# Three attention loops by pairs: differential maps subtracted and turned once, indexed and latent values stationary in column halves

## What is computed

```python
# even mixer: indexed attention "a", 8 heads of 64; sel = keys the indexer chose
s = where(valid, q @ k.T * d ** -0.5, -inf)
a = softmax(s) @ v * silu(ag)
r = head_group_norm(retention(q, k, bv)) * silu(bg)      # 4 heads of 128
out = concat([a, r]) @ w_out
# odd mixer: differential "c", 4 heads, two maps each (q, k 64; v 128)
o = causal_attention(qs, ks, concat([v, v]), C_QK_DIM ** -0.5)
c = rms_norm(o[:4] - lam * o[4:], subln) * (1.0 - lam_init) * silu(cg)
# latent "m", 8 heads (q, k 96; v 64)
m = causal_attention(q_full, k_full, kv[..., 64:], 96 ** -0.5) * silu(dg)
out = concat([c, m]) @ w_out
```

## Time and profile before

| | us |
|---|---|
| median of three runs | 2604.29 |
| lowest, highest | 2601.57, 2605.11 |
| span of the profiled execution | 2599.6 |
| PE busy in it | 2539.9 (98%) |
| DVE busy | 1311.2 (50%) |
| ACT busy | 657.8 (25%) |
| indexed loop | 127.6 to 283.6 |
| differential loop | 467.0 to 547.4 |
| latent loop | 549.9 to 632.7 |

### The profile page before, as it was taken

The page is one execution under the profiler, slowest core; times in us unless marked ns, Lnnn a source line. Parts: engine busy times, 40 slices in busy tenths (PEclk is TensorE's granted clock), DMA queues, the critical chain, the costliest instruction groups (busy, mean ns, idle before and its releaser), DMA issues.

```text
span 2599.6 us, 31517 instructions
## 1 busy us (share of the span) xinstructions
PE 2539.9 (98%) x12699; PEld 1731.9 (67%) x12699; DVE 1311.2 (50%) x2535; ACT 657.8 (25%) x1485; POOL 60.1 (2%) x116
## 2 busy tenths in 40 slices
PE   8999999999999999999999999999999999999999
PEld 3487557566588888744545745555555775888886
DVE  6765342544544456424464346657473544344564
ACT  2123232364300000133344042525344002000001
POOL 0000000000000000000000010101020000000000
PEclk9999999999999999999999999999999999999999
DMA  4111222000232221221111221212112321322221
GB/s 159 65 65 66 77 87 85 33 33 33 65 97 65 97 97 67 79 97 53 47 66 68 81 81 65 72 42 82 66 49 100 120 97 65 97 69 94 98 78 69
DMA packets 121032, 196.86 MB, mean 76 GB/s; under 512 B 5212, under 2 KB 61336, under 8 KB 119992
## 3 DMA queue, kind: packets, MB, share of 16 engines
q1 hardware_dynamic: 118848, 180.52, 20.4%
q0 software_dynamic: 1344, 12.19, 1.2%
q10 hardware_dynamic: 696, 2.13, 0.2%
HBM read 187.49 MB, written 7.34 MB: 75 GB/s over the span
## 4 chain that ended last, share of the span: by engine, by line
PE 94%; DVE 3%; ACT 2%; issue 1%; DMA 0%; ACTq 0%; SPq 0%; DVEq 0%
PE psum L542 22%; PE psum L539 15%; PE psum L2503 10%; PE psum L2485 8%; PE psum L422 7%; PE psum L407 6%; PE psum L444 4%; PE psum L2537 3%; PE psum L461 2%; PE psum L1249 2%; PE psum L1229 1%; PE psum L468 1%; PE psum L395 1%; PE psum L1237 1%; PE psum L2429 1%
## 5 line engine op out<-in xcount | busy, mean ns | idle before, releaser
L595 DVE TENSOR_TENSOR arena<-arena,psum 128x512 f32<-128x512 f32 x197 | 135.3, 687 | 357.8 <-PE psum L542 304.5
L2503 PE MATMUL psum<-weight_ring,h_t 128*128 128x512 f32 x640 | 291.4, 598 | 0.5 <-issue 0.5
L542 PE MATMUL psum<-h_t,weight_ring 128*128 128x256 f32 x1120 | 250.2, 379 | 1.2 <-DVE h_t L736 1.0
L542 PEld LDWEIGHTS psum<-h_t,weight_ring 128*128 128x128 f32 x1120 | 212.4, 190 | 30.9 <-issue 2.2
L2485 PE MATMUL psum<-h_t,weight_ring 128*128 128x512 f32 x512 | 232.1, 595 | 0.3 <-issue 0.3
L539 PE MATMUL psum<-weight_ring,arena 128*128 128x256 f32 x992 | 220.5, 379 | 1.5 <-ACT arena L2962 1.5
L539 PEld LDWEIGHTS psum<-weight_ring,arena 128*128 128x128 f32 x992 | 188.3, 190 | 27.9 <-issue 2.4
L2503 PEld LDWEIGHTS psum<-weight_ring,h_t 128*128 128x128 f32 x640 | 116.4, 192 | 116.7 <-issue 115.6
L422 PE MATMUL psum<-h_t,weight_ring 128*128 128x512 f32 x416 | 180.1, 593 | 1.2 <-DVE arena L3215 1.0
L542 PE MATMUL psum<-arena 128*128 128x256 f32 x768 | 169.7, 379 | 0.0
L407 PE MATMUL psum<-weight_ring,h_t 128*128 128x512 f32 (+1 forms) x384 | 163.8, 582 | 0.8 <-ACT arena L2042 0.7
(11 more groups left out here) (439 smaller groups left out, 3409.9 us busy)
## 6 DMA issues: line engine op xcount, KB each, us to landing
weight_ring<-in_ffn_w_in_dram SPq DMA_DIRECT2D x44, 1024.0 KB, 7.4
weight_ring<-in_w_in_dram SPq DMA_DIRECT2D x20, 2048.0 KB, 7.9
weight_ring<-in_ffn_w_out_dram SPq DMA_DIRECT2D x8, 2048.0 KB, 7.7
weight_ring<-in_w_in_even_dram SPq DMA_DIRECT2D x7, 2048.0 KB, 8.3
weight_ring<-in_w_in_odd_dram SPq DMA_DIRECT2D x5, 2048.0 KB, 7.9
weight_ring<-in_w_in_dram SPq DMA_DIRECT2D x8, 1024.0 KB, 7.0
weight_ring<-in_w_branch_gdn_dram SPq DMA_DIRECT2D x4, 2048.0 KB, 7.9
weight_ring<-in_ffn_w_out_dram SPq DMA_DIRECT2D x4, 1536.0 KB, 6.7
```

Of the source, the lines that this page charges most:

```text
L542: ins = pe.matmul(out, w, right[:, k, :], start=first, stop=last)
L595: ins = dve.tensor_tensor(out, other, bank, op)
L2503: last = pe.matmul(bank, act[:, k, t * P:(t + 1) * P], slot[:, k, :], start=(k == 0), stop=(k == KD - 1))
```

## The change

The three loops go by pairs: 16 steps of two maps (`pe_pairs`, `act_pairs`, `dve_pairs`). Both maps are scored, masked and exponentiated; then DVE (`weigh`) divides them by their sums before they are turned. Transposes and values of pair m-2 stand in iteration m.

- `mask(m, r)` on DVE waits for the scores and for the transposes of pair m-2, whose slots it writes.
- In c a pair is the two maps of one head. DVE subtracts them with one instruction, scaled so that one division of the output remains; one map is turned and one multiplied. The subtraction of outputs (L2192) goes.
- In a and m a pair is two heads. Both maps are scaled over nk columns and turned. For the values v is stationary, 64 columns wide, in one column half per head, and the turned map moves, 128 columns; the output comes with features on the partitions. ACT copies it out for the first 12 (a) or 14 (m) pairs, DVE the rest. The outputs of a and m are no longer turned; ag and dg are produced by feature too (stationary and moving swapped in the same stream).
- The output projections read tiles from a list. Even: n_first is 3, the retention's four tiles are turned in between. Odd: n_first is 4, the last four tiles wait for the dg gate, which comes after the loop. The norm's squares are taken at pairs 3 and 4, eight each, the square root at pair 5; both of heads 0 and 1 must be copied before m begins. Fill: 2 half steps of seven in a, 2 or 3 matmuls in c, 2 in each of 12 pairs in m.

The core of the diff; the removed lines of the old functions, which stand above, are left out in most places.

```diff
+
+
+def pe_pairs(K, pe, tag, steps, bufs, beside, behind=None):
+
+    slots, turned = bufs
+    n_steps, base = len(steps), K.pair_base[tag]
+    for m in range(n_steps + 2):
+        i = m - 2
+        if i >= 0:
+            step, kept = steps[i], 2 * (i % 2)
+            pe.wait_ge(K.weights_ready, base + i + 1)
+            for r in range(step["heads"]):
+                bank = pe_fresh(K, pe, (tag, "t", i, r))
+                for kb in range(step["nk"] // P):
+                    last = pe.transpose(bank[:, kb * P:(kb + 1) * P], slots[:, kept + r, kb * P:(kb + 1) * P], K.const("ident"))
+                last.then_inc(K.full_of((tag, "t", i, r)), 1)
+        if m < n_steps:
+            step = steps[m]
+            banks = [pe_fresh(K, pe, (tag, "s", m, r)) for r in range(2)]
+            for r in range(2):
+                pe.matmul(banks[r][:, 0:step["nk"]], step["q"][r], step["k"][r], start=True,
+                          stop=True).then_inc(K.full_of((tag, "s", m, r)), 1)
+        if m <= n_steps:
+            beside(m)
+        if i >= 0:
+            step = steps[i]
+            bank, nkb = pe_fresh(K, pe, (tag, "o", i)), step["nk"] // P
+            for r in range(step["heads"]):
+                pe.wait_ge(K.free_of((tag, "t", i, r)), K.turn((tag, "t", i, r)))
+            for kb in range(nkb):
+                ks = slice(kb * P, (kb + 1) * P)
+                if step["heads"] == 1:
+                    last = pe.matmul(bank[:, 0:P], turned[:, 0, ks], step["v"](kb), start=(kb == 0), stop=(kb == nkb - 1))
+                else:
+                    for r in range(2):
+                        last = pe.matmul(bank[64 * r:64 * r + 64, 0:P], step["v"](kb, r), turned[:, r, ks],
+                                         start=(kb == 0), stop=(kb == nkb - 1))
+            last.then_inc(K.full_of((tag, "o", i)), 1)
+        if behind:
+            behind(m)
+    beside(n_steps + 1)
...
+def act_pairs(K, act, tag, steps, bufs, ahead, beside, evicted=0):
+
+    slots, turned = bufs
     n_steps, base = len(steps), K.att_base[tag]
+    for n in range(n_steps + 3):
+        i = n - 3
+        if 0 <= i < evicted:
+            act.wait_ge(K.full_of((tag, "o", i)), K.turn((tag, "o", i)))
+            act.copy(steps[i]["out"], K.bank((tag, "o", i))[:, 0:P]).then_inc(K.free_of((tag, "o", i)), 1)
+        ahead(n)
+        i = n - 2
+        if 0 <= i < n_steps:
+            nk = steps[i]["nk"]
+            if i:
+                act.wait_ge(K.full_of((tag, "o", i - 1)), K.turn((tag, "o", i - 1)))
+            for r in range(steps[i]["heads"]):
+                act.wait_ge(K.full_of((tag, "t", i, r)), K.turn((tag, "t", i, r)))
+                act.copy(turned[:, r, 0:nk], K.bank((tag, "t", i, r))[:, 0:nk]).then_inc(K.free_of((tag, "t", i, r)), 1)
+        if n < n_steps:
+            nk = steps[n]["nk"]
+            for r in range(2):
+                c = 2 * n + r
+                part = slots[:, 2 * (n % 2) + r, 0:nk]
+                act.wait_ge(K.scores_masked, base + c + 1)
+                act.activation(part, part, ACT.Exp, bias=K.stat[:, 20 + c % 4:21 + c % 4], scale=steps[n]["scale"],
+                               accum_out=K.stat[:, 24 + c % 8:25 + c % 8]).then_inc(K.probs_ready, 1)
+        beside(n)
...
+def dve_pairs(K, dve, tag, steps, bufs, beside, finish):
+
+    slots, _ = bufs
...
+    def weigh(i):
+        step, c = steps[i], 2 * i % 8
+        nk, kept = step["nk"], 2 * (i % 2)
+        dve.wait_ge(K.probs_ready, base + 2 * i + 2)
+        dve.reciprocal(K.stat[:, 32 + c:34 + c], K.stat[:, 24 + c:26 + c]).then_inc(K.one_more("dve"), 1)
+        dve.wait_ge(K.steps["dve"], K.step_n["dve"])
+        first, second = slots[:, kept, 0:nk], slots[:, kept + 1, 0:nk]
+        if step["heads"] == 1:
+            ratio = K.stat[:, 40 + i % 4:41 + i % 4]
+            dve.tensor_scalar(ratio, K.stat[:, 24 + c:25 + c], K.stat[:, 33 + c:34 + c], K.lam[:, 4:5], ALU.mult,
+                              ALU.mult).then_inc(K.one_more("dve"), 1)
+            dve.wait_ge(K.steps["dve"], K.step_n["dve"])
+            dve.scalar_tensor_tensor(first, second, ratio, first, ALU.mult, ALU.add).then_inc(K.weights_ready, 1)
+        else:
+            dve.tensor_scalar(first, first, K.stat[:, 32 + c:33 + c], None, ALU.mult).then_inc(K.one_more("dve"), 1)
+            dve.tensor_scalar(second, second, K.stat[:, 33 + c:34 + c], None, ALU.mult).then_inc(K.weights_ready, 1)
+
+    for n in range(n_steps + 3):
+        if n >= 3:
+            finish(n - 3)
         if n < n_steps:
+            mask(n, 0)
+            mask(n, 1)
+        if 1 <= n <= n_steps:
+            weigh(n - 1)
+        beside(n)
...
+def even_pairs(K, V):
+    for c in range(A_H // 2):
+        for i in range(NT):
+            nk = (i + 1) * P
+            steps.append(dict(q=[V["aq_t"][p:p + 64, c, i * P:nk] for p in (0, 64)],
+                              k=[V["ak_t"][p:p + 64, c, 0:nk] for p in (0, 64)], nk=nk, heads=2,
+                              v=lambda kb, r, c=c: V["av"][:, kb, (2 * c + r) * 64:(2 * c + r + 1) * 64],
+                              scale=A_D ** -0.5, out=V["mixed"][:, c, i * P:nk]))
...
+    pe_pairs(K, pe, "a", even_pairs(K, V), V["pairs"], lambda m: half_step(2 * m), lambda m: half_step(2 * m + 1))
+
+    def rest():
+        for i in range(12, 16):
+            pe.wait_ge(K.free_of(("a", "o", i)), K.turn(("a", "o", i)))
+        pe.wait_ge(K.mixed_ready, 4)
+        for kt in range(4, KD):
             pe_mixed(K, pe, s, V["mixed"], kt)
+        for kt in range(4, KD):
             pe.wait_ge(K.free_of((s, "mixed", kt)), K.turn((s, "mixed", kt)))
 
+    pe.wait_ge(K.mixed_ready, 3)
     ahead = pe_odd_ahead(K, pe, "odd", s)
+    pe_square_early(K, pe, (s, "out"), tiles_of(V["mixed"][:, :, 0:512]) + tiles_of(K.h_t)[4:KD], 3, rest, pe_next_norm(K, pe, s, True, ahead))
     pe.drain().then_inc(K.phase_met, 1)
...
-                ins = pe.matmul(bank[:, q * HALF:(q + 1) * HALF], right[:, k, q * P:(q + 1) * P], left[:, k, :],
+                still, moving = (right, left) if token_major else (left, right)
+                ins = pe.matmul(bank[:, q * HALF:(q + 1) * HALF], still[:, k, q * P:(q + 1) * P], moving[:, k, :],
...
+        if n % 4 and n < 16:
+            act_even_stream(K, act, s, V, n // 4, 2 * n % 8)
+
+    def beside(n):
+        half_step(2 * n)
+        half_step(2 * n + 1)
+
+    act_pairs(K, act, "a", even_pairs(K, V), V["pairs"], ahead, beside, 12)
...
+        for i in range(4 * kt, 4 * kt + 4):
             dve.wait_ge(K.free_of(("a", "o", i)), K.turn(("a", "o", i)))
+        m = V["mixed"][:, kt, 0:512]
+        dve.tensor_tensor(m, m, V["ag"][:, kt, :], ALU.mult).then_inc(K.mixed_ready, 1)
+
+    def beside(n):
+        half_step(2 * n)
+        half_step(2 * n + 1)
+
+    steps = even_pairs(K, V)
+
+    def finish(i):
+        if i >= 12:
+            key = ("a", "o", i)
+            dve.wait_ge(K.gates_ready, 1)
+            dve.wait_ge(K.full_of(key), K.turn(key))
+            dve.tensor_tensor(steps[i]["out"], K.bank(key)[:, 0:P], V["ag"][:, 3, (i - 12) * P:(i - 11) * P],
+                              ALU.mult).then_inc(K.free_of(key), 1)
+
+    dve_pairs(K, dve, "a", steps, V["pairs"], beside, finish)
...
-        if m < 4 * 2 * C_H:
-            pe_take(fill, 2 if m % 4 == 3 else 1)
+        if m < NT * C_H:
+            pe_take(fill, 2 + m % 2)
...
+        if m < 12:
+            pe_take(fill, 2)
         K.banks_in_turn = SIDE_BANKS
+        h = 2 * (m // 4) + 2 + m % 4 // 2
+        if m % 2 == 0 and h < M_H:
             pe_transpose(K, pe, (s, "q_t", h), lambda t: V["qd"][:, t, h * M_Q:(h + 1) * M_Q], M_Q)
             pe_transpose(K, pe, (s, "k_t", h), lambda t: V["k_full"][:, t, h * M_Q:(h + 1) * M_Q], M_Q)
+        if m % 4 == 3 and m < 12:
+            for n in range(2):
+                heads_there(h - n)
+        if m in (14, 15):
+            pe.wait_ge(K.odd_mixed, 1)
+            for kt in (2 * m - 28, 2 * m - 27):
+                pe_mixed(K, pe, s, V["mixed"], kt)
         K.banks_in_turn = LOW_BANKS
 
+    for h in range(2):
+        heads_there(h)
+    pe_pairs(K, pe, "m", mla_pairs(K, V), V["pairs"], beside_mla)
+
+    def gated():
+        pe.wait_ge(K.odd_mixed, 5)
+
+    for kt in range(4):
         pe.wait_ge(K.free_of((s, "mixed", kt)), K.turn((s, "mixed", kt)))
     ahead = pe_ffn_ahead(K, pe, "ffn1", s)
+    pe_square_early(K, pe, (s, "out"), tiles_of(K.h_t)[0:4] + tiles_of(V["ao"]), 4, gated, pe_next_norm(K, pe, s, True, ahead))
...
+    def ahead_mla(n):
+        h = 2 * (n // 4) + 2 + n % 4 // 2
+        if n % 2 == 1 and h < M_H:
+            for name in ("q_t", "k_t"):
+                key = (s, name, h)
+                act.wait_ge(K.full_of(key), K.turn(key))
+                act.copy(V[name][0:M_Q, h % 4, :], K.bank(key)[0:M_Q, :]).then_inc(K.free_of(key), 1)
+        if n in (15, 16):
+            for kt in (2 * n - 30, 2 * n - 29):
+                act_mixed(K, act, s, kt)
```

(32 more changed lines are left out.)

285 lines of the change are left out of this document (67 added, 218 removed).

## The result

The changed kernel takes 2573.27 us, median of its runs, against 2604.14 for the kernel before. The ratio is 0.9881, with a 95% interval of 0.9867 to 0.9894: 31 us less. The forecast was 2579, range 2564 to 2593. The profiled execution has a span of 2571.0 us, 28.6 less than before.

A forecast was written before the change was run, and what follows sets the result against it. TensorE (PE), busy 98% of the span, was taken to bind. Differential loop -10, even mixer (indexed loop and tail) -8.3, latent loop -7 sum to -25.3 us, off the 2604.3 median: 2579, range 2564 to 2593.

The forecast's parts named there:

- Differential loop: Odd mixer: 40 transposes and 40 value matmuls fewer, -13.3 us, less new waits and lost fill; net -10, bounds -12 and -6.
- Indexed loop: Even mixer: values -4.9, old waits and low clock gone -5.2, new waits and low clock +7.8; net -2.3 us.
- the price of the halves: Indexed and latent loops: value passes in alternating column halves at .054 us each plus .15 for entering; -4.9 us per loop.
- Even tail: Before and in the even projection: 16 transposes and their wait go, -4.3, low clock -1.7; -6.0 us, last gate's chain covered.
- Latent loop: Odd mixer, with its tail: values -4.9, outputs not turned -2.7, old waits -7.4, new ones +9.5, starting gaps -1.5; -7 us.
- the waits that went (-7.4): Latent loop: 5.7 us of old waits, 4.6 of it for exponentials, and 1.7 of low clock disappear.
- Elsewhere: Everything outside the named loops and tails costs nothing: same passes in the same number, 0 us.
- Rival 1: All 48 iterations: DVE ahead of PE binds, 1.1 us more lost in each, 53 us, 2632; chance 0.02 in full.
- Rival 2: Indexed and latent loops: column halves don't overlap, +6.5 us in each, 2592; chance 0.14.
- Rival 3: The three loops: of 18.6 us of added waits and low clock, 12 don't come, 2567; chance 0.14.
- Rival 5: Indexed and latent loops: PSUM eviction binds, 1 us in each of 32 iterations, 2611; chance 0.02 in full.
- Rival 4: Latent loop's end and retention: three more low-clock stretches of 1.7 us, +5, 2584; chance 0.12, within the forecast's 0.56.

The follow-up runs named there:

- c_both_turned: The changed kernel with both maps of the differential loop scaled, turned and multiplied into one bank, subtracted by accumulation in PSUM; 2584.65 us, ratio 0.9926.
- scaling_twice: The changed kernel with the indexed and latent loops' maps passed over twice more on DVE, times 1.0; 2581.02 us, ratio 0.9912.
- halves_in_turn: The changed kernel with one head's value passes all before the other's in the indexed and latent loops, so column halves don't alternate; 2581.45 us, ratio 0.9913.
- fill_over_16: The changed kernel with the latent loop's 24 fill matmuls spread over 16 pairs instead of 12, three ACT evictions later; 2577.32 us, ratio 0.9898.
- turned_twice: The changed kernel with the retention's four tiles turned twice in the even tail, 16 transposes more; 2576.19 us, ratio 0.9897.
- head_0_by_act: The changed kernel with ACT instead of DVE copying head 0's turned query and key before the latent loop; 2568.52 us, ratio 0.9865.
- squares_over_4: The changed kernel with the latent loop's squares in four lots of four (pairs 3 to 6), square root at pair 6; 2570.94 us, ratio 0.9875.

## Why the prediction was right, and where its terms were off

The time, 2573.3, lies in the stated range, at the edge of the forecast's own 2573 to 2586. The five stretches of the two mixers, by the profiles, gave -25.8 for a forecast of -25.3. The mechanism held (passes taken away on PE, against new waits), but that the sum is so close is luck in part: the indexed loop came out 2.6 worse and four others .2 to 1.5 better.

**Differential loop, forecast -10, measured -11.5.** The passes (-13.3) were right; c_both_turned gives 13.5 without waits and low clock. What I added to that, 3.2, came to 1.8, with .5 of low clock in it that I hadn't put there: five short ones for the subtraction, 1.5 in all, took the place of the small ones before, and .8 for the last map's copy and a second wait, of 1.08 beside the old one of 1.2, are as I had put them.

**Indexed loop, forecast -2.3, measured +.25** (155.98 before its last values' end at 283.63, 156.23 after). The waits I named came, at 3.0 and 1.4 us for 3.2 and 1.7, and .8 and .9 at the end for .7 in all; the low clock came too. The step that failed most is the price of the halves. From the earlier trace rows I took .15 for entering a group, which is the cost behind it only. There is one in front as well: in the rows of the latent loop above, four fill passes in front of values in halves take 1.82 us (546.49 to 548.31), and in front of whole-array transposes 1.72 (551.58 to 553.30). A tenth of a microsecond in each of 16 groups is 1.5 us per loop, so the values' gain was 3.4, not 4.9. Another .6 is in the waits that went: I took 3.5, and the list of waits has 2.9. The remaining .4 or so isn't assigned. The Trainium skill (TensorEngine Tiling (Array Packing), Key Properties) says that a change of tiling mode drains TensorE; the trace agrees, at about .1 us a change. In the Trainium skill the section Performance Considerations of the same page gives the swap with 2x column tiling; a gain of 2x in time is not reached here: 16.0 us of values became 11.1 and 1.5.

**Even tail, forecast -6.0, measured -6.9.** The 4.3 between the loop and the projection went (values end and the projection starts at 284.02), the low clock in the projection went, and .9 more went further on in this stretch that I had not looked at, .7 of it a wait at L407 for ACT (L2042). The cover of the last gate held: the wait at the second part is .93, as before.

**Latent loop, forecast -7, measured -7.7 with its tail.** The squares and the square root cost 1.8 for my 3.7. The last four pairs cost about 5.3 by the distances in the timeline, for 4.9. The low clock at the loop's start, 2.1, I had placed in the tail at half a chance, .9. The price in front of the halves holds here too, 1.5 us that I had not counted. My terms for the outputs, 1.75 and .8, make 2.6 and not the 2.7 that I wrote; the tail's share of them, 1.7, came to 1.9. By all these the loop should have come out 1.2 us worse than forecast where it came out .7 better. So 1.9 us aren't assigned; they lie in the terms that no run isolates, the waits that went (-7.4) and the smaller starting gaps (-1.5).

**Elsewhere, forecast 0, measured -2.9**: pauses of 7.0 us before and 2.0 after, less 1.7 of low clock and .4 of waits. No term of the forecast has this, and nothing of it is known to be the change's doing. By the medians the change gained 30.9, 2.3 more than by the spans of the two profiled executions.

**Rivals.** Rival 1 (DVE ahead of PE binds) is refuted by scaling_twice. Rival 2 (no overlap) is refuted by the sixteen passes in 1.02 us; with the halves in turn, which still overlap by half, the latent loop's values took 3.0 us more. Rival 3 (few new waits) was wrong in its reason, though the time lies between it and my forecast. Rival 5 (eviction binds) is true at two pairs, for 1.8 us, and fill_over_16 shows how near the loop is to it. Rival 4 happened in part.

## What to carry to other kernels

Take away passes on the bound engine first, and price a change of array tiling on both sides of a group. When work is moved ahead of a wait on another engine, look for what stands behind it in that engine's queue and feeds a third one: reordering DVE by one block was worth 1.5 us of waits, splitting four copies between two engines 1.4. The medians, 3.5 and 4.8, showed more than twice that. Judge small edits by the stretches of the trace between fixed groups, and first take off the low clock in them, by the same stretch of a profile that has none. Otherwise two edits can both claim the same stretch of low clock, as here, and their sum comes out too large. Runs of one kernel differed by up to 8 us with their granted clock (turned_twice, 0.999 to 0.995).

## What the runs showed of the hardware

- A whole-array group next to one in column halves pays about .1 us, in front and behind, beside the mean of .055 us a pass: by the starts in turned_twice's trace a transpose is followed by another after .11 us and by a pass in halves after .20, a pass in halves by a whole-array one after .20. Scores of 64 rows cost the same next to whole-array passes; scores of 96 rows don't.
- Passes in the same column half start .11 us apart, like whole-array ones. In alternating halves two start nearly together every .11 us; that is the .055 (the change). With one half after the other (halves_in_turn), the second half's first pass starts .46 us into the group, beside the fifth of eight.
- The indexed loop had, behind the same wait of 3.0 us, 3.4 us of low clock in three kernels' profiles (the change, head_0_by_act, squares_over_4), at a cost of 1.6 us, 6.8 us of it in one (halves_in_turn) and none in three (c_both_turned, fill_over_16, turned_twice). Further on, waits at 1079, 1296 and 1530 us did and did not have it. Ahead of the end of the kernel its stretches lasted 3.4 or 6.8 us.
- PE paused without a semaphore wait by 1.9 to 2.6 us: three times in the kernel before (up to 705.6, 1179.6 and 1323.4 us), twice in turned_twice, not at all in c_both_turned, and once, near 1290 us, in the others. Each stands in the middle of a run of like matmuls.
